# A gather of the expert tables is issued only when the fourth gather ahead of it in the stream has landed

## The chip, the core and the metric

One core of one Trainium2 chip. The metric is the device time of one execution in microseconds. The kernel before took 3083.66 us (median of three runs, 3082.61 to 3083.81).

## What is computed

One layer of a diffusion backbone over 1024 latent tokens of width 1024, with 256 context tokens. A token mixer (attention with 8 heads and a bidirectional recurrent group) is followed by a channel mixer that retrieves single-neuron experts from two tables of 16384 rows of 1024 float32 values, `u` and `v`. Eight heads pick 16 experts each, so 128 rows of each table for every token:

```python
idx = jnp.take_along_axis(cand_i, pos, axis=-1)          # (128 tokens, 8 heads, 16)
g = jax.nn.softmax(top_s, axis=-1)
act = jax.nn.gelu(jnp.einsum('nhkd,nd->nhk', u[idx], xc))
return jnp.einsum('nhk,nhkd->nd', g * act, v[idx])
```

Everything is float32. The layer works on the tokens in 8 chunks of 128.

## The kernel before

The program is written engine by engine, with semaphores set by hand. SP loads and stores plain data. DVE, ACT and PE do the mixer of chunk c + 2 while the experts of chunks c + 1 and c are gathered and used. Once the prelude is over, POOL (GpSimd) does nothing but issue gathers.

A gather (`gather`, L618) is an indirect DMA that takes one row of 4 KB for each of 128 partitions, 524 KB in all, into one place of `ring`, which has `RING` = 11 places. For each chunk there are 128 gathers from `u` and 128 from `v`, 2048 in all, and they form one stream with fixed places:

- a **u gather** j brings the j-th expert of each of the 128 tokens. DVE multiplies it by the tokens and sums along the row (`u_slots`, L1561, one product of 128 x 1024 at L1565);
- a **v gather** j brings the 128 experts of one token, one on each partition. ACT makes a column of weights for it (L960), PE multiplies and adds it into PSUM (`v_slots`, L2092, matmuls at L2100).

The order of the stream is set by `u_place` and `v_place`: for chunk 0 first its 128 u gathers; then for each chunk c 60 v gathers in a row (`lead_gathers`, `LEAD` = 60), then a mixed stretch (`mixed_gathers`) of 16 blocks of twelve, each with 8 u gathers of chunk c + 1 and 4 v gathers of chunk c (`RUN` = 4), then 4 v gathers (`TAIL`). For the last chunk all 128 v gathers stand in a row.

Each ring place r has a semaphore `got[r]`, which a gather raises by 16 when it has landed. DVE and PE wait on it in `landed` (L315). In the other direction DVE raises `u_used` and PE `v_used` for each gather that was used. Ahead of each gather POOL calls `freed` (L638), which waits until the gather 11 places earlier in the stream was used. A gather is issued as soon as that has happened and POOL has finished the one before; how many are in flight at once is limited by the ring alone. Ahead of the first u gather of each half chunk and the first v gather of each chunk POOL also waits for the indices and raises `passed`.

On DVE and PE the uses are woven into the attention work of a later chunk by hand: the mixer code calls `fill(b)` at fixed points, and `fill` runs the uses up to a given place. Both engines work strictly in the written order. So a use that waits for its gather holds up the attention work behind it, and attention work holds up the uses behind it and with them the ring places that these would free.

Of the kernel before, what the change touches and what calls it, by code (L numbers as in the profile page):

```python
# [54 lines left out]
SLOTS = PH * TOPK  # L55
HALF_SLOTS = SLOTS // 2
RING = 11
QUADS, QP = 4, 32
SELS = 8
LABEL = 2 * NK  # L60
# [5 lines left out]
STRIDE = 2 * SLOTS  # L66
# [42 lines left out]
def layer(nc, t):  # L109
    with ExitStack() as ctx:  # L110
# [3 lines left out]
        def sem(name):  # L114
            return ctx.enter_context(nc.semaphore(name))
# [31 lines left out]
        def view(n, *dims):  # L147
            assert at[0] + n <= ARENA, at[0] + n
            a = arena[:, at[0]:at[0] + n]
            at[0] += n  # L150
            if dims:
                names = "abcd"[:len(dims)]
                a = a.rearrange("p (%s) -> p %s" % (" ".join(names), " ".join(names)),
                                **dict(zip(names, dims)))
            return a
# [72 lines left out]
        wo = view(KT * D, KT, D)  # L228
        ring = view(RING * D, RING, D)
        xm_new, xm_next, xm_cur = (view(D) for _ in range(3))  # L230
# [84 lines left out]
        def landed(eng, c, place):  # L315

            r = slot(c, place)
            eng.wait_ge(got[r], 16 * ((c * STRIDE + place) // RING + 1))
            return r

        def slot(c, place):

            return (c * STRIDE + place) % RING

# [28 lines left out]
            "ffn_sd", "ffn_out",  "out_ready", "out_stored")}  # L353
        got = [sem(f"got{r}") for r in range(RING)]

# [210 lines left out]
        def _(pool):  # L566
# [55 lines left out]
            def u_gather(c, j):  # L622

                if j % HALF_SLOTS == 0:
                    pool.wait_ge(S["idx_ready"], 2 * c + j // HALF_SLOTS + 1)
                    pool.sem_inc(S["passed"], 1)
                freed(c, u_place(c, j))
                gather("u", idx_u, j, slot(c, u_place(c, j)))

            def v_gather(c, j):  # L630

                if j == 0:
                    pool.wait_ge(S["idxT_copied"], c + 1)
                    pool.sem_inc(S["passed"], 1)
                freed(c, v_place(c, j))
                gather("v", idx_v[c % 2], token(j), slot(c, v_place(c, j)))

            def freed(c, place):  # L638

                place -= RING  # L640
                first, last = isinstance(c, int) and c == 0, isinstance(c, int) and c == NX - 1
                if first and place < SLOTS:
                    if place >= 0:
                        pool.wait_ge(S["u_used"], place + 1)
                    return
                if place < SLOTS:
                    c, place = c - 1, place + STRIDE
                    last = False
                n = place - SLOTS - LEAD
                if n < 0 or last:  # L650
                    pool.wait_ge(S["v_used"], c * SLOTS + LEAD + n + 1)
                elif n >= MIXED:
                    pool.wait_ge(S["v_used"], c * SLOTS + SLOTS - TAIL + n - MIXED + 1)
                elif n % (3 * RUN) >= 2 * RUN:
                    j = LEAD + RUN * (n // (3 * RUN)) + n % (3 * RUN) - 2 * RUN
                    pool.wait_ge(S["v_used"], c * SLOTS + j + 1)
                else:
                    j = 2 * RUN * (n // (3 * RUN)) + n % (3 * RUN)
                    pool.wait_ge(S["u_used"], c * SLOTS + (SLOTS + j + 1))
# [1033 lines left out]
        def _(pe):  # L1693
# [267 lines left out]
            def spread(b, r, ready):  # L1961

                for i in range(2):
                    ins = M(bank(b + i), lhsT=ident[r:r + 1, r:r + 1].broadcast_to([1, P]),  # L1964
                            rhs=rows[r:r + 1, 512 * i:512 * i + 512], start=True, stop=True)
                ins.then_inc(S[ready], 1)
# [125 lines left out]
            def v_slots(c, lo, hi):  # L2092

                for j in range(lo, hi):
                    q, i = j % QUADS, j // QUADS
                    pe.wait_ge(S["sel_ready"], c * SLOTS + j + 1)
                    r = landed(pe, c, v_place(c, j))
                    for b in range(2):
                        g = (q + 2 * b) % QUADS
                        ins = M(bank(4 + b)[QP * g:QP * g + QP, :], lhsT=sel[:, j % SELS, :],  # L2100
                                rhs=ring[:, r, 512 * b:512 * b + 512], start=(i == 0), stop=(i == QP - 1))
                    ins.then_inc(S["v_used"], 1)
# [85 lines left out]
            spread(0, G2, "g2_ready")  # L2188
            v_slots(NX - 1, G2_AT, SLOTS - RING)
            pe.wait_ge(S["out_ready"], NX - 1)  # L2190
# [55 lines left out]
```

## Time and profile before

| | |
|---|---|
| median of the runs shown | 3083.66 us |
| span of the profiled execution | 3447.3 us |
| POOL busy in the span | 2087.7 us (61%) |
| PE busy | 2466.8 us (72%) |
| DVE busy | 2047.0 us (59%) |
| ACT busy | 785.3 us (23%) |
| read from HBM and written to it | 337 GB/s over the span |

The profiled execution is longer than the unprofiled ones by 363.6 us. All rows of the trace are from that one execution. In a timeline row the first number is the start in us from the span's start, the second the length, and the bracket at the end gives the engine's idle time just before the instruction and what ended it. "remote" there is a release whose sender the trace does not name; "issue" means that no wait shows. DMA landings have no rows of their own, but a DVE or PE row with "<-DMA" started when its gather had landed.

### The profile page before, as it was taken

Reading aid. Unit: us, or ns where it says so; the run is one execution under the profiler, and the core shown is the slowest. Engines: PE = TensorE matmul, PEld = TensorE weight load, DVE = VectorE, ACT = ScalarE, POOL = GpSimd, SP = SyncE. Lnnn points to the kernel's source line nnn. Section 1 sums busy time; section 2 is a strip of 40 time slices with the busy share of each in tenths; the row PEclk is TensorE's granted clock in tenths of the full one; section 3 lists DMA queues with packets and bytes.
Section 4 is the critical chain, followed back from the end, with each engine's and each line's share of the span. In section 5 each row is a group of like instructions: output and inputs, shape, how many; then the busy total and the mean of one; then the engine's idle time right before and its main releaser. Section 6 shows DMA issues by size and latency. Waiting matters only on the chain.

```text
span 3447.3 us, 29321 instructions
## 1 busy us (share of the span) xinstructions
PE 2466.8 (72%) x9222; PEld 1078.6 (31%) x9222; DVE 2047.0 (59%) x4621; ACT 785.3 (23%) x1888; POOL 2087.7 (61%) x2167
## 2 busy tenths in 40 slices
PE   7978977768676776677777867787767766533476
PEld 4844654324221432134222422143213422000011
DVE  4785786666655666656656566665665666565300
ACT  2265111122112221222122221222122212100121
POOL 6910254566666666666666666666666666666665
PEclk8989987886789667865797578956796688855699
DMA  8533499799999999999999999999999999999998
GB/s 319 179 140 113 142 337 358 288 358 362 349 371 367 360 364 367 362 368 358 364 367 375 361 364 372 372 358 366 364 361 370 361 355 359 372 379 368 364 367 323
DMA packets 335937, 1163.76 MB, mean 338 GB/s; under 512 B 40485, under 2 KB 51365, under 8 KB 333608
## 3 DMA queue, kind: packets, MB, share of 16 engines
q0 software_dynamic: 297792, 1084.36, 83.6%
q1 hardware_dynamic: 37994, 77.54, 6.3%
q8 instruction: 76, 1.25, 0.1%
q14 instruction: 75, 0.61, 0.0%
HBM read 1148.13 MB, written 13.63 MB: 337 GB/s over the span
## 4 chain that ended last, share of the span: by engine, by line
PE 29%; POOL 16%; issue 14%; another core or an unknown queue 13%; DMA 12%; DVE 11%; ACT 4%; SPq 1%; DVEq 0%; ACTq 0%; POOLq 0%
POOL arena L619 16%; DMA arena<-in_v,arena 9%; PE psum L2100 9%; DVE arena L1565 6%; PE psum L1931 4%; PE psum L1899 4%; DMA arena<-in_u,idx_u 2%; PE psum L2034 2%; PE psum L1920 2%; PE psum L1946 2%; PE psum L1781 1%; PE psum L1956 1%; PE psum L1980 1%; ACT arena L883 1%
## 5 line engine op out<-in xcount | busy, mean ns | idle before, releaser
L1565 DVE CUSTOM_DVE_ANT_0 arena<-arena,psum 128x1024 f32<-128x1024 f32 x1024 | 1215.6, 1218 | 413.3 <-DMA arena<-in_u,idx_u 379.4
L619 POOL DMA_INDIRECT arena<-in_u,idx_u x1024 | 960.0, 937 | 652.8 <-issue 267.8
L2100 PE MATMUL psum<-arena 128*32 128x512 f32 x4096 | 1013.0, 744 | 445.6 <-DMA arena<-in_v,arena 305.4
L619 POOL DMA_INDIRECT arena<-in_v,arena x1024 | 977.6, 955 | 522.1 <-issue 256.8
L2100 PEld LDWEIGHTS psum<-arena 128*32 128x32 f32 x4096 | 181.8, 124 | 1185.3 <-issue 1036.6
L960 ACT ACTIVATE arena<-arena 128x32 f32<-128x32 f32 x1024 | 277.6, 314 | 1166.4 <-PE psum L2100 580.1
L1899 PE MATMUL psum<-kT,arena 64*128 64x512 f32 (+1 forms) x384 | 252.4, 810 | 56.2 <-issue 26.9
L1920 PE MATMUL psum<-ident,arena 128*128 128x128 f32 x560 | 137.5, 378 | 174.5 <-issue 110.3
L1401 DVE TENSOR_REDUCE small<-psum 128x1 f32<-128x1280 f32 x64 | 95.4, 1491 | 278.4 <-remote 220.8
L1931 PE MATMUL psum<-v,arena 128*128 128x64 f32 x1120 | 230.4, 395 | 27.3 <-ACT arena L883 24.0
L2034 PE MATMUL psum<-wbig,arena 128*128 128x512 f32 x512 | 242.4, 628 | 4.5 <-issue 3.4
L1931 PEld LDWEIGHTS psum<-v,arena 128*128 128x128 f32 x1120 | 221.4, 304 | 45.4 <-ACT arena L883 38.5
L883 ACT ACTIVATE arena<-psum 128x512 f32<-128x512 f32 x168 | 87.9, 523 | 403.6 <-remote 287.1
L1920 PEld LDWEIGHTS psum<-ident,arena 128*128 128x128 f32 x560 | 82.7, 186 | 296.6 <-issue 196.6
L1899 PEld LDWEIGHTS psum<-kT,arena 64*128 64x128 f32 x384 | 100.7, 279 | 185.7 <-issue 147.7
L2034 PEld LDWEIGHTS psum<-wbig,arena 128*128 128x128 f32 x512 | 100.7, 202 | 142.1 <-issue 140.3
L1426 DVE TENSOR_SCALAR small<-small 128x1 f32<-128x1 f32 x24 | 3.6, 152 | 225.8 <-ACT arena L977 164.4
L1964 PE MATMUL psum<-rows,ident 1*128 1x512 f32 x128 | 60.2, 824 | 77.9 <-issue 42.7
L1980 PE MATMUL psum<-arena 128*128 128x512 f32 x224 | 115.0, 668 | 0.0
L826 ACT ACTIVATE arena<-psum,small 128x64 f32<-128x64 f32 x64 | 20.0, 313 | 309.0 <-remote 197.5
L819 ACT ACTIVATE arena<-psum,small 128x1280 f32<-128x1280 f32 x64 | 84.8, 1325 | 23.6 <-issue 13.2
L1565 DVE DVE_READ_ACCUMULATOR2_ANT arena<- 128x1 f32 x1024 | 84.6, 83 | 0.0
(268 smaller groups left out, 2154.9 us busy)
## 6 DMA issues: line engine op xcount, KB each, us to landing
arena<-in_u,idx_u POOLq DMA_INDIRECT x1024
arena<-in_v,arena POOLq DMA_INDIRECT x1024
arena<-in_w_mod POOLq DMA_DIRECT2D x20, 512.0 KB, 4.3
wbig<-in_wq SPq DMA_DIRECT2D x1, 7168.0 KB, 19.7
arena<-in_w_mod SPq DMA_DIRECT2D x12, 512.0 KB, 4.1
arena<-in_xin SPq DMA_DIRECT2D x5, 1024.0 KB, 9.6
arena<-in_w_mod SPq DMA_DIRECT2D x2, 2048.0 KB, 10.7
wbig<-in_w_mod SPq DMA_DIRECT2D x2, 2048.0 KB, 20.5
```

The lines of the kernel that those rows point to most:

```text
L619: pool.indirect_dma_start(ring[:, r, :], None, t[table], bass.IndirectOffsetOnAxis(idx[:, j:j + 1], 0)).then_inc(got[r], 16)
L819: A(pr, psum[:, score_at(n):score_at(n) + KEYS], ACT.Exp, scale=HD ** -0.5, bias=small[:, a:a + 1], accum_out=small[:, b:b + 1]).then_inc( ...
L883: A(pT[:, 4 * g:4 * g + k, :], bank(3)[:, 0:k * P], ACT.Copy).then_inc(S["pt_out"], 1)
L960: A(sel[:, j % SELS, :], hot[:, QP - 1 - i:2 * QP - 1 - i], ACT.Copy, scale=wT[:, n:n + 1])\
L1401: ch.link(V.tensor_reduce(small[:, a:a + 1], psum[:, score_at(n):score_at(n) + KEYS], AX, ALU.max))
L1565: V.tensor_tensor_reduce(ring[:, r, :], ring[:, r, :], hx_cur, 1.0, 0.0, ALU.mult, ALU.add, act_[:, j:j + 1]).then_inc(S["u_used"], 1)
L1899: ins = M(psum[:, at_ + b:at_ + b + w], lhsT=qc[o:o + 64, h // 2, :], rhs=kT[o:o + 64, b:b + w], start=True, stop=True)
L1920: ins = T(bank(3)[:, j * P:(j + 1) * P], pr[:, kt * P:(kt + 1) * P], ident[:, :])
L1931: ins = M(pv, lhsT=pT[:, kt, :], rhs=v[:, kt, 64 * (h % 2):64 * (h % 2) + 64], start=(kt == 0), stop=(kt == NTOK - 1))
L1980: return M(bank(i), lhsT=att[:, kt, :] if kt < 4 else lc[:, kt - 4, :], rhs=wo[:, kt, 512 * i:512 * i + 512], start=(kt == 4), stop=(kt == 3))
L2034: ins = M(bank(i), lhsT=hxT[:, kt, :], rhs=wq[:, kt, 512 * i:512 * i + 512], start=(kt == 0), stop=(kt == KT - 1))
L2100: ins = M(bank(4 + b)[QP * g:QP * g + QP, :], lhsT=sel[:, j % SELS, :], rhs=ring[:, r, 512 * b:512 * b + 512], start=(i == 0), stop=(i == ...
```

## The change

`freed` gets one wait more, at its head. `before` is the place in the stream of the gather four places ahead of the one to be issued, and POOL waits until the semaphore of its ring place says that it has landed. The wait for the ring place 11 earlier stays as it is. Nothing else changes: order, ring size, and all consumers stay.

```diff
 RING = 11
+FLIGHT = 4
 QUADS, QP = 4, 32
@@
             def freed(c, place):
 
+                before = c * STRIDE + place - FLIGHT
+                if before >= 0:
+                    pool.wait_ge(got[before % RING], 16 * (before // RING + 1))
                 place -= RING
```

## Rows read from the trace of the kernel before

**Rows 1.** The page: span, and busy time of each engine with its share.
```profile
span 3447.3 us, 29321 instructions
...
PE 2466.8 (72%) x9222; PEld 1078.6 (31%) x9222; DVE 2047.0 (59%) x4621; ACT 785.3 (23%) x1888; POOL 2087.7 (61%) x2167
```

**Rows 2.** DMA, 374 to 3447 us: gathers' queue, packets, MB, share of 16 engines.
```profile
q0 software_dynamic: 294912, 1073.87, 92.7%
```

**Rows 3.** Groups of instructions: busy us, mean ns of one, idle before, releaser.
```profile
L619 POOL DMA_INDIRECT arena<-in_u,idx_u x1024 | 960.0, 937 | 652.8 <-issue 267.8
...
L619 POOL DMA_INDIRECT arena<-in_v,arena x1024 | 977.6, 955 | 522.1 <-issue 256.8
```

**Rows 4.** Waits: who waited for what, us in total, times, longest us.
```profile
DVE arena L1565 <- DMA arena<-in_u,idx_u: 379.4, 95, 9.6
...
POOL arena L619 <- PE psum L2100: 259.6, 171, 20.1
...
POOL arena L619 <- remote: 187.2, 82, 4.9
...
POOL arena L619 <- DVE arena L1565: 148.5, 116, 23.1
```

**Rows 5.** Timeline of POOL, 1989 to 2008 us, a block of the mixed stretch.
```profile
1989.80 0.93 POOL L619 DMA_INDIRECT arena<-in_u,idx_u  x1 [0.30 <-issue]
...
1997.25 0.94 POOL L619 DMA_INDIRECT arena<-in_u,idx_u  x1 [0.30 <-issue]
2000.94 0.94 POOL L619 DMA_INDIRECT arena<-in_u,idx_u  x1 [2.75 <-remote]
2002.18 0.94 POOL L619 DMA_INDIRECT arena<-in_v,arena  x1 [0.30 <-issue]
...
2007.15 0.94 POOL L619 DMA_INDIRECT arena<-in_u,idx_u  x1 [0.30 <-issue]
```

**Rows 6.** Timeline of DVE, 1996 to 2015 us: uses of the u gathers.
```profile
1996.29 1.22 DVE L1565 CUSTOM_DVE_ANT_0 arena<-arena,psum 128x1024 f32<-128x1024 f32 x1 [3.54 <-issue]
...
2005.38 1.22 DVE L1565 CUSTOM_DVE_ANT_0 arena<-arena,psum 128x1024 f32<-128x1024 f32 x1 [0.42 <-DMA arena<-in_u,idx_u]
...
2013.62 1.22 DVE L1565 CUSTOM_DVE_ANT_0 arena<-arena,psum 128x1024 f32<-128x1024 f32 x1 [7.01 <-DMA arena<-in_u,idx_u]
...
2014.90 1.22 DVE L1565 CUSTOM_DVE_ANT_0 arena<-arena,psum 128x1024 f32<-128x1024 f32 x1
```

**Rows 7.** Timelines of POOL and PE from 3419 us: the last gathers and their uses.
```profile
3419.36 0.94 POOL L619 DMA_INDIRECT arena<-in_v,arena  x1 [1.88 <-PE psum L2100]
3420.60 0.94 POOL L619 DMA_INDIRECT arena<-in_v,arena  x1 [0.30 <-issue]
...
3430.53 0.94 POOL L619 DMA_INDIRECT arena<-in_v,arena  x1 [0.30 <-issue]
...
3426.27 1.05 PE L2100 MATMUL psum<-arena 128*32 128x512 f32 x4 [1.30 <-DMA arena<-in_v,arena]
...
3436.78 1.05 PE L2100 MATMUL psum<-arena 128*32 128x512 f32 x4 [0.18 <-DMA arena<-in_v,arena]
```

**Rows 8.** Timeline of POOL: the second gather, and one behind two waits.
```profile
375.40 0.96 POOL L619 DMA_INDIRECT arena<-in_u,idx_u  x1 [0.30 <-issue]
...
2133.44 0.94 POOL L619 DMA_INDIRECT arena<-in_v,arena  x1 [0.30 <-issue]
```

**Rows 9.** Timelines of POOL and DVE, 962 to 973 us: a lone gather.
```profile
962.02 0.94 POOL L619 DMA_INDIRECT arena<-in_u,idx_u  x1 [0.30 <-issue]
967.80 0.93 POOL L619 DMA_INDIRECT arena<-in_u,idx_u  x1 [4.85 <-PE psum L2100]
...
972.10 1.22 DVE L1565 CUSTOM_DVE_ANT_0 arena<-arena,psum 128x1024 f32<-128x1024 f32 x1 [2.75 <-DMA arena<-in_u,idx_u]
```

**Rows 10.** DMA packets, 1996 to 2001 us, then 2003.5 to 2009 us.
```profile
DMA packets 575, 2.09 MB, mean 419 GB/s; under 512 B 64, under 2 KB 64, under 8 KB 575
...
DMA packets 451, 1.65 MB, mean 300 GB/s; under 512 B 48, under 2 KB 48, under 8 KB 451
```

## The prediction

> **What bounds the kernel now.** Read the totals first. POOL, which only issues gathers from 374 us on, is busy 61% of the span, PE 72%, DVE 59% [rows 1]: none of them is full. The DMA engines are: from 374 us to the end the gathers' queue moves 1073.87 MB and occupies 92.7% of the sixteen engines [rows 2]. That is 2048 gathers of 524 KB. The groups of instructions say that POOL spends 0.94 us on one [rows 3], and the timeline shows 0.30 us between two, so POOL can issue one in 1.243 us (1989.80 to 1997.25 is six of them, 1.242 each [rows 5]). The first issue is at 374.03 (1.37 us before the second [rows 8]), the last at 3430.53 [rows 7], so the mean spacing is 3056.5 / 2047 = 1.493 us. The other 0.25 us each, some 510 us in all, are stalls. The waits name them: POOL waited 259.6 us for PE, 187.2 us for a release without a name and 148.5 us for DVE [rows 4], 595.3 us with the usual 0.30 us before each of those 369 issues in it. They are waits for a free place in the ring of 11.
>
> So two things take turns: the ring that comes free late, and the DMA. What the DMA does between stalls decides this case.
>
> **How many gathers are in flight now.** This is read off by pairing issues with first uses. In the block shown, eight u gathers start at 1989.80 and later, the eighth at 2000.94 after a stall of 2.75 us, then four v gathers from 2002.18, then the next block at 2007.15 [rows 5]. DVE takes the u gathers in order: the first at 1996.29, the eighth at 2005.38, the first of the next block at 2013.62 [rows 6]. From issue to use that is 6.49 us, 4.44 us and 6.47 us. At the end of the stream PE uses every v gather as it lands: the last is issued at 3430.53 and used at 3436.78, 6.25 us [rows 7]. At 1.243 us spacing 6.25 us are 5.0 gathers between issue and use. The change allows four. So it binds wherever POOL runs freely: use of the fourth gather ahead is 6.25 us after its issue, and four spacings are 4.97 us. Only after a stall (4.44 us) is it already fulfilled.
>
> **What the change removes, adds and moves.** It removes nothing. It adds one wait on POOL ahead of 2044 of the 2048 gathers. *The instruction itself:* the second gather, which waits for nothing, starts 0.30 us after the one before it ended; the gather at 2133.44, the first v gather of a chunk, stands behind two waits and a semaphore increment, all fulfilled, and starts 0.30 us after too [rows 8]. A fulfilled wait therefore costs nothing that shows. Bounds 0 and 0.06 us; I take 0: POOL has 0.25 us per gather to spare, which covers it.
>
> *The wait when it is not fulfilled:* the spacing cannot be below a quarter of the time from issue to the moment when POOL sees the landing. I take the time to the consumer's start for that, since POOL wakes on the same semaphore as DVE and PE. From below: a gather with next to nothing ahead of it, issued at 967.80, 5.78 us after the one before it, is used at 972.10, 4.30 us later [rows 9]; 4.30 / 4 = 1.08 us, less than POOL's own 1.243, so the wait would cost nothing. From above: 6.25 / 4 = 1.56 us. In between the queue decides: fewer gathers ahead, less time. The gather issued at 3420.60, second after a stall and so with two to three ahead of it, is used at 3426.27, 5.67 us [rows 7] (nine issues and nine uses from there to the end, one for one). That is the state the cap keeps, three ahead, so I take 5.67 / 4 = **1.42 us**.
>
> Does the DMA lose speed there, or does it merely wait less? In a free run use follows use at 1.28 us (2013.62 to 2014.90), but from the eighth u gather (2005.38) to the ninth (2013.62), five gathers, 8.24 us pass, 1.65 each, though POOL issued these every 1.24 us [rows 5, 6]. The DMA rate says the same: 419 GB/s from 1996 to 2001 us, 300 GB/s from 2003.5 to 2009 [rows 10]. With two gathers ahead of a new one the sixteen engines aren't kept full; with four or five they are. Three is between, and the mean of 1.65 and 1.28, 1.46, is near the 1.42 above.
>
> **Queues behind the wait.** Behind POOL's wait stand only further gathers. DVE's products (u) and PE's sums (v) wait for them, and behind these the attention work of the chunk two ahead. DVE already waited 379.4 us for u gathers [rows 4], so a later u gather delays it directly. A v gather's release of its ring place follows the landing, so POOL's ring waits move too.
>
> **The sum, against the profiled execution.** Span 3447.3 = 374.0 before the stream + 3056.5 + 16.8 after. In the mixed stretches (16 blocks of twelve in each of seven chunks, 112 blocks) a block takes 2007.15 - 1989.80 = 17.35 us now. Capped, twelve spacings of 1.42 are 17.04 us: POOL's stall of 2.45 us at its end would swallow all of it. But the eight u gathers come later one after the other by up to 8 x (1.42 - 1.243) = 1.4 us, and DVE takes them as they land. With half of that passed on, 0.7 us x 112 = **+78 us**; bounds 0 and +157.
>
> The median is 3083.66 us, 363.6 less than the span. Nothing shows where the difference lies; if outside the stream nothing changes, the unprofiled spacing is (3083.66 - 390.8) / 2048 = 1.315 us, and if everything shrinks alike, 1.493 x 0.8945 = 1.336 us. Either is so near the 1.28 of the free run that few stalls can be left to hide the cap. Then the cost is (1.42 - 1.336) x 2048 = **+172 us** to (1.42 - 1.315) x 2048 = **+215 us**, mean 194. I put the forecast midway between 78 and 194, +136 us: **3220 us**, own range 3110 to 3300.
>
> **Rivals.**
> *The DMA stays full (no change).* For it: in the worst trough it is still at 300 GB/s, and a lone gather needs 4.30 us, of which four in flight make 1.08 us. Then 1.243 and not the cap sets the spacing, 3084 us. Against it: 6.25 us is what a gather takes in a free run, and 1.65 spacing after a stall. A variant is that the change does nothing, because four are never exceeded; the 5.0 above speaks against it.
> The Trainium skill, "DMA: Bandwidth & Descriptors", section "Anatomy of one DMA — SWDGE (gpsimd) path", gives 2.0 us + bytes / 436 GB/s for such a transfer. By it a gather would take an estimated 3.2 us and four in flight would allow one in 0.8 us: it would make this rival the forecast. The trace's lone gather, 4.30 us to its use, is longer, and its 6.25 us in a free run is longer still.
>
> *Evenness (faster).* Today a stall drains the queue and the next five gathers take 8.24 us where 5 x 1.28 = 6.4 would do. If POOL, held back evenly, arrives at the release with less run ahead and the trough goes, up to 1.8 us a block come back; 112 x 1.8 = 206 us at most in the profiled execution, of which the unprofiled spacing leaves about a fifth, 40 us: 3044 us. It needs the trough to come from POOL's burst; but the trough follows a release time set by PE, which the cap doesn't move. It decides only if the capped spacing is under 1.31 us.
>
> *Latency doesn't fall with the queue (much slower).* Then 1.56 us: (1.56 - 1.336) x 2048 = +459 us at most, 3543 us; a half-way case at 1.47 gives +274, 3358 us. For it: gathers issued a little after a stall are back at 6.2 us soon (the one at 2007.15). Against it: those had caught up to four ahead again.
>
> **Chances and range.** Forecast 0.63; much slower 0.11; DMA full or no effect 0.15; faster 0.11. A difference of 0.2% (6 us) is about what a measurement of this kernel can tell from none, so faster 0.11, same 0.15, slower 0.74. The range leaves out the faster case below 3080 and the much slower one above 3350.
>
> **What would show it.** After: POOL's idle before L619 put down to the DMA, in hundreds of us; spacing of free runs 1.40 to 1.45 instead of 1.243, issue to use 5.6 to 5.8 instead of 6.25; DVE's wait for u gathers up; the DMA's share and GB/s from 374 us on down by 3 to 6%; ring waits on PE shorter. If instead free runs stay at 1.25 to 1.28 and the last gather is used about 5.2 us after its issue, the DMA stayed full with a shorter queue and the forecast is wrong. It is also wrong if time from issue to use is shorter when nothing is profiled: at 5.3 us the cap gives 1.33, no cost.

## The result

The change made the kernel **18.4% slower**: 3649.32 us (median of four runs, 3647.93 to 3651.09) against 3083.31 us, ratio 1.1835 with a 95% interval of 1.182 to 1.1849. The forecast was 3220 us, with 3080 to 3350 as its range. The direction was right, and the size was wrong by a factor of four: +566 us, not +136.

One thing has to be said before any number is compared. The chips used here fall into two groups. On one kind the kernel before takes 3079 to 3087 us, on the other 3421 to 3452 us. Going by these numbers, the times of before are from the first kind, and the profile shown ahead of the prediction (span 3447.3) is from the second. The experiments e1 and e17 below show that a profiled execution takes what the other executions on its chip take. The trace of the changed kernel, and below a second trace of the kernel before (span 3082.4), are from the first kind. I call them 3082-chips and 3440-chips. The experiments used three of the first (labels e5 to e8, e13 to e16, e17 and e18) and two of the second (e1 to e4, e9 to e12); each was used for one set of runs only, so whether a chip always stays in its group is not known.

The traces of the two kinds differ in one thing more. Those of the 3082-chips record nearly every update that a DMA makes to a semaphore (35225 in e17). Those of the 3440-chips record well under half (12496 in the profile ahead of the prediction, 13249 in e1). So on a 3440-chip a release can lack a name ("remote") because its record is missing, and waits put down to a DMA are counted too low there. The times at which POOL issued are complete in both.

The profile after: gathers (L620 is L619 of before), with POOL's idle time and what ended it.

```profile
L620 POOL DMA_INDIRECT arena<-in_u,idx_u x1024: 932/936/1881, 374.9 to 3419.3; - x171
L620 POOL DMA_INDIRECT arena<-in_v,arena x1024: 932/936/2127, 619.2 to 3632.0; - x171
its engine sat idle before it (us, times) until:
  DMA arena<-in_u,idx_u: 566.7, 826
  DMA arena<-in_v,arena: 555.2, 871
...
DMA to landing us min/median/max: 4.2/6.0/15.4
```

The numbers after x1024 are the shortest, median and longest issue in ns and the first and last start. POOL spent 0.94 us on an issue as before [rows 3], so it isn't slower at its work. But the idle time before 1697 of 2048 issues is put down to a landing, 1121.9 us in all. Each of them contains the usual 0.30 us, 509 us together, so some 610 us are really lost to landings. Before, no issue waited for a landing. The last line gives the time from a gather's issue to its last landing.

The same view of the kernel before on a 3082-chip (label e17):

```profile
L619 POOL DMA_INDIRECT arena<-in_u,idx_u x1024: 935/941/1887, 374.9 to 2890.7; - x171
L619 POOL DMA_INDIRECT arena<-in_v,arena x1024: 935/941/1926, 598.6 to 3062.3; - x171
its engine sat idle before it (us, times) until:
  issue: 461.7, 1515
  DVE arena L1565: 153.7, 267
  PE psum L2100: 129.7, 265
...
DMA to landing us min/median/max: 4.3/9.7/24.7
```

From first to last issue the spacing is (3062.3 - 374.9) / 2047 = 1.313 us before and (3632.0 - 374.9) / 2047 = 1.591 us after. The difference, 0.278 x 2047 = 569 us, is the result. Outside the stream little moved: the first issue is at 374.9 in both, and after the last issue 17.0 us follow instead of 20.1. And the kernel before had 9.7 / 1.313 = 7.4 gathers in flight, not five.

The users waited more, too (the waits of after: DVE and PE for gathers):

```profile
DVE arena L1569 <- DMA arena<-in_u,idx_u: 893.4, 485, 7.6
...
PE psum L2104 <- DMA arena<-in_v,arena: 809.0, 596, 14.0
```

DVE's wait was 379.4 us in the trace ahead of the prediction [rows 4] and is 465.1 us in e17; PE's is 425.7 us in e17. The DMA in both, from 374 us to the end, first e17, then after (packets and rate, and the gathers' queue):

```profile
DMA packets 304901, 1098.44 MB, mean 406 GB/s; under 512 B 33664, under 2 KB 36736, under 8 KB 304768
...
q0 software_dynamic: 294912, 1073.87, 98.0%
```

```profile
DMA packets 304916, 1098.56 MB, mean 335 GB/s; under 512 B 33664, under 2 KB 36736, under 8 KB 304768
...
q0 software_dynamic: 294912, 1073.87, 91.5%
```

The same bytes at 335 instead of 406 GB/s. The share of the engines fell far less than the rate, from 98.0% to 91.5%. The rest is in the packets, which took longer: by these lines 98.0% of 16 engines over 2708 us for 294912 packets make 144 ns each, and 91.5% over 3275 us make 163 ns. So a high busy share of the DMA is no proof that it runs at its full rate.

A free run of POOL in the kernel before (e17) and a stretch of the mixed part of after, as timelines:

```profile
1803.27 0.94 POOL L619 DMA_INDIRECT arena<-in_u,idx_u  x1 [0.30 <-issue]
1804.51 0.94 POOL L619 DMA_INDIRECT arena<-in_u,idx_u  x1 [0.30 <-issue]
1805.76 0.94 POOL L619 DMA_INDIRECT arena<-in_v,arena  x1 [0.30 <-PE psum L2100]
```

```profile
2329.72 0.94 POOL L620 DMA_INDIRECT arena<-in_u,idx_u  x1 [0.30 <-DMA arena<-in_v,arena]
2331.96 0.94 POOL L620 DMA_INDIRECT arena<-in_u,idx_u  x1 [1.30 <-DMA arena<-in_v,arena]
2333.29 0.94 POOL L620 DMA_INDIRECT arena<-in_u,idx_u  x1 [0.40 <-DMA arena<-in_u,idx_u]
2334.80 0.94 POOL L620 DMA_INDIRECT arena<-in_u,idx_u  x1 [0.57 <-DMA arena<-in_u,idx_u]
2336.05 0.94 POOL L620 DMA_INDIRECT arena<-in_u,idx_u  x1 [0.30 <-DMA arena<-in_u,idx_u]
2337.64 0.94 POOL L620 DMA_INDIRECT arena<-in_u,idx_u  x1 [0.66 <-DMA arena<-in_u,idx_u]
```

Before, one issue follows another after 1.24 us. After, the gap of 0.30 us is often 0.4 to 1.3, five issues in 7.92 us, 1.58 each, and each gap ends with a landing.

### The profile page after: what moved, and what is told of

Same layout as the page of the kernel before. It is cut to its first block, busy times and chain, and to the rows that moved or that the text cites. A ratio compares the mean times of both kernels' runs of the same rounds, so it can differ in the third digit from the quotient of the medians.

```text
span 3649.0 us, 31358 instructions
## 1 busy us (share of the span) xinstructions
PE 2485.4 (68%) x9222; PEld 965.9 (26%) x9222; DVE 2069.8 (57%) x4621; ACT 830.0 (23%) x1888; POOL 2091.9 (57%) x2167
## 3 DMA queue, kind: packets, MB, share of 16 engines
q8 instruction: 76, 1.25, 0.1%
## 4 chain that ended last, share of the span: by engine, by line
DMA 28%; POOL 27%; issue 21%; PE 11%; DVE 11%; ACT 2%; SPq 1%; POOLq 1%; DVEq 0%; ACTq 0%
POOL arena L620 27%; DMA arena<-in_u,idx_u 21%; DVE arena L1569 8%; DMA arena<-in_v,arena 6%; PE psum L2104 2%; PE psum L1785 2%; PE psum L2038 2%; PE psum L1950 1%; PE psum L1960 1%; PE psum L1903 0%; SPq L383 0%; PE psum L1722 0%; PE psum L1890 0%; DMA arena<-in_k_norm_g 0%; PE psum L1984 0%
## 5 line engine op out<-in xcount | busy, mean ns | idle before, releaser
L2104 PE MATMUL psum<-arena 128*32 128x512 f32 x4096 | 1211.0, 754 | 839.8 <-DMA arena<-in_v,arena 809.0
L1569 DVE CUSTOM_DVE_ANT_0 arena<-arena,psum 128x1024 f32<-128x1024 f32 x1024 | 1239.6, 1220 | 905.5 <-DMA arena<-in_u,idx_u 893.4
L620 POOL DMA_INDIRECT arena<-in_u,idx_u x1024 | 960.0, 937 | 738.8 <-DMA arena<-in_u,idx_u 337.6
L620 POOL DMA_INDIRECT arena<-in_v,arena x1024 | 982.2, 959 | 633.4 <-DMA arena<-in_v,arena 311.6
L964 ACT ACTIVATE arena<-arena 128x32 f32<-128x32 f32 x1024 | 314.5, 319 | 1635.5 <-PE psum L2104 1635.0
L2104 PEld LDWEIGHTS psum<-arena 128*32 128x32 f32 x4096 | 193.9, 120 | 1785.6 <-issue 1216.5
L1903 PE MATMUL psum<-kT,arena 64*128 64x512 f32 (+1 forms) x384 | 211.0, 698 | 52.6 <-ACT arena L823 51.4
L1935 PE MATMUL psum<-v,arena 128*128 128x64 f32 x1120 | 153.3, 298 | 26.9 <-ACT arena L887 26.9
L1935 PEld LDWEIGHTS psum<-v,arena 128*128 128x128 f32 x1120 | 145.5, 211 | 40.5 <-ACT arena L887 39.1
L1924 PE MATMUL psum<-ident,arena 128*128 128x128 f32 x560 | 112.8, 324 | 54.6 <-ACT arena L887 35.7
L1903 PEld LDWEIGHTS psum<-kT,arena 64*128 64x128 f32 x384 | 86.9, 242 | 160.6 <-issue 100.1
L1924 PEld LDWEIGHTS psum<-ident,arena 128*128 128x128 f32 x560 | 68.2, 159 | 144.9 <-issue 75.9
```

Of the source, the lines that this page charges most:

```text
L620: pool.indirect_dma_start(ring[:, r, :], None, t[table], bass.IndirectOffsetOnAxis(idx[:, j:j + 1], 0)).then_inc(got[r], 16)
L964: A(sel[:, j % SELS, :], hot[:, QP - 1 - i:2 * QP - 1 - i], ACT.Copy, scale=wT[:, n:n + 1])\
L1569: V.tensor_tensor_reduce(ring[:, r, :], ring[:, r, :], hx_cur, 1.0, 0.0, ALU.mult, ALU.add, act_[:, j:j + 1]).then_inc(S["u_used"], 1)
L1903: ins = M(psum[:, at_ + b:at_ + b + w], lhsT=qc[o:o + 64, h // 2, :], rhs=kT[o:o + 64, b:b + w], start=True, stop=True)
L1924: ins = T(bank(3)[:, j * P:(j + 1) * P], pr[:, kt * P:(kt + 1) * P], ident[:, :])
L1935: ins = M(pv, lhsT=pT[:, kt, :], rhs=v[:, kt, 64 * (h % 2):64 * (h % 2) + 64], start=(kt == 0), stop=(kt == NTOK - 1))
```

## The experiments

**Theory A:** the stream is a loop. A gather is issued when the one F ahead has landed, so F x spacing = time from issue to last landing + the time POOL needs to react. **Theory B:** the added wait costs POOL time at each gather. **Theory C:** late gathers delay the attention work on DVE and PE, and that work delays the stream.

### How the two times of before go together: e1 and e17

No edit.

> The kernel before, unchanged. It asks how long a profiled execution of it takes by its own clock, since the profile shown spans 3447 us while its runs take 3083, and the changed kernel's span and runs are both 3649. If the profiler slows a stream with many gathers in flight, this profile again spans over 3400 us and the run takes 3083. If the profile shown was an accident, the span is near 3083.

> The kernel before. Where it takes 3082 us: spacing 1.27 us in the bulk, some 120 intervals over 1.3 us, 6.2 to 6.5 us from issue to landing, POOL's waits for PE released without delay. Where it takes 3440: a third copy of the profile shown.

e1 took 3444.64 us with a span of 3442.8, beside seven runs of the kernel before of 3421 to 3452; e17 took 3084.25 us with a span of 3082.4. So neither of e1's expectations about the profiler held: a profiled execution takes what a run takes, and the chips differ. In e17 the issues came as expected (110 intervals over 1.3 us), but the time from issue to landing, 9.7 us, was far over the 6.2 to 6.5 expected. On the 3440-chip of the first trace the intervals between issues exceed 1.243 us by 515 us in sum, in e17 by 144 us. POOL's named waits for PE, DVE and unnamed senders were 595.3 us there [rows 4] and are 283.4 us in e17 (129.7 for PE and 153.7 for DVE). In the record of semaphore updates of the 3440-chips, PE's releases of several v gathers often come together, 0.06 us apart: four at 2000.68 to 2000.86, of matmuls that began between 1995.73 and 1998.29, and POOL's issue at 2000.94 [rows 5] follows. In that trace 344 of 920 recorded releases by PE come less than 0.15 us after the one before, in e17 58 of 1024. From the start of a gather's last matmul to the next recorded release it is 1.9 us in the median there and 0.61 us in e17. Why PE's releases are late there, no run here shows. That the slow chips are also the ones whose traces lose records leaves open that recording and slowness have one cause; every execution here has its span recorded, so none can tell.

### The limit: e2, e3, e4, e8, e9, e13, e14, e15, e18, e5

```diff
-FLIGHT = 4
+FLIGHT = 3        # and 5, 6, 8, 11
```

> Five instead of four gathers in flight. Theory A (spacing = time from issue to POOL's sight of the landing, divided by the gathers allowed): with four allowed that time is 4 x 1.57 = 6.3 us; with five it is at most 6.3 + 0.6, so 1.26 to 1.38 us of spacing against 1.315 before: 3040 to 3220 us, most likely 3110. Theory B (the added wait costs POOL time at each gather, whatever it waits for): again near 3649 us. Theory C (the cost grows slowly with the limit because engines drift apart): 3300 to 3400 us.

> Eight in flight. Theory A: 6.9 / 8 = 0.9 us, no bound: within 0.3% of 3083 us. Theory B: near 3649 us. A third possibility, that deep queues are needed to fill holes after PE's stalls, gives 3100 to 3150 us.

> Eleven in flight: the wait is for the gather whose ring place is reused, whose use POOL waits for anyway, so it is always fulfilled when its turn to count comes. It prices the instruction alone. Theory A: within 0.2% of 3083 us (0 to 6 us). Theory B: 3649 us. If a fulfilled wait costs POOL 0.06 us and POOL were the bound, 3083 + 0.06 x 2048 = 3206 us.

> The changed kernel (four in flight) again, unchanged. Its own runs were 3649 us beside 3083 us for the kernel before, but on the chip of the second set of experiments the kernel before takes 3446. If the chip slows every gather alike, this takes 3649 x 3446 / 3083 = 4079 us. If only a deep queue is slower on that chip and a stream held to four in flight is bound by time from issue to landing, it takes 3630 to 3670 us on either chip.

> Three in flight. If the spacing is the loop from issue over landing to next issue divided by the number allowed, 6.26 us now with four; with three the queue is shorter by one (0.3 to 0.6 us), so 5.7 to 6.0 us / 3 = 1.9 to 2.0 us: 390 + 2048 x 1.95 = 4380 us (4280 to 4490). If the DMA's speed falls with a shorter queue further than that, over 4490; if the cost is mainly one of the wait, 3700 to 3800.

> Five in flight again, since the first time the kernel before took 3446 us on that chip. Where it takes 3082 us: theory A (spacing = loop from issue over landing to the next issue, over the number allowed; 5.64 us with three, 6.36 with four): about 6.9 / 5 = 1.38 with the same growth, less as the engines fill up; the kernel before has 1.274 in the bulk. 3100 to 3220 us, most likely 3140. If the cost of a separate wait instruction ahead of the ring releases were the main thing, three, four and five would cost alike. If the chip is the slow kind again, 3506.

> The changed kernel. Where the kernel before takes 3082 us: 3645 again. Where it takes 3440: theory A says that the capped stream is bound by its own loop of 6.3 us, which needs neither PE nor DVE, so again 3630 to 3700 us. If everything is slower there, about 4070 us.

> Five in flight. Where the kernel before takes 3082 us: 3100 to 3220 us, most likely 3140 (loop of 6.6 to 6.9 us over five, 1.32 to 1.38 us of spacing). Where it takes 3440: 3507 as twice before.

> Eleven in flight, the ring wait as an instruction of its own. Where the kernel before takes 3082 us there are few stalls on the ring (119 intervals over 1.3 us in the trace of the swapped kernel, against 249 on the other kind), so 0.38 us at each is at most 45 us, and the queue that is full hides most of it: 3083 to 3105 us. Where it takes 3440: 3508 again.

> Six in flight. Where the kernel before takes 3082 us: loop of 7.0 us over six is 1.17 us, under POOL's own 1.243, so within 0.3% of 3083 us. Where it takes 3440: 3507, as five and eight.

On 3082-chips, with spacing from first and last issue and the median from issue to last landing:

| gathers in flight | time us | ratio to before (95%) | spacing us | x limit us | issue to landing us |
|---|---|---|---|---|---|
| 3 (e8) | 4239.03 | 1.375 (1.3722 to 1.3777) | 1.880 | 5.64 | 5.2 |
| 4 (e13) | 3646.58 | 1.1831 (1.1811 to 1.185) | 1.590 | 6.36 | 6.0 |
| 5 (e14) | 3159.89 | 1.0257 (1.024 to 1.0274) | 1.352 | 6.76 | 6.0 |
| 6 (e18) | 3096.64 | 1.0043 (1.0026 to 1.006) | 1.320 | 7.92 | 7.2 |
| 11 (e15) | 3083.78 | 1.0006 (0.9996 to 1.0016) | 1.312 | - | 9.2 |
| no limit (e17) | 3084.25 | the kernel before | 1.313 | - | 9.7 |

e5 gave 3644.67 us with four (1.182, 1.1801 to 1.184), on another chip than e13. Theory B falls: with eleven the same instructions stand in the program and nothing is lost. Theory A holds at three and four: the loop is the landing time (5.25 and 5.97 us) plus 0.39 us. The semaphore record gives the reaction itself: in the changed kernel POOL's issue follows the last landing by 0.259 us, from the fifth percentile to the median; the rest is issues that waited for something else or for POOL's own 1.24 us. At five the loop binds part of the time, at six hardly. I had expected 3140 us for five (3159.89 measured) and 3083 for six (3096.64, outside the 0.3% given), 4280 to 4490 for three (4239.03, below): the direction of the growth is right, but the landing time jumps between three and four and again after five, which a straight line through it doesn't have.

More on it is in the semaphore record. A landed gather has raised its semaphore by sixteen single updates, one for each of the sixteen DMA engines. In medians after the issue, in us (without the first 200 gathers, 1847 in each trace):

| limit | first engine | 15th | last engine |
|---|---|---|---|
| 3 (e8) | 3.84 | 5.06 | 5.25 |
| 4 (after) | 4.19 | 5.71 | 5.97 |
| 6 (e18) | 4.99 | 6.63 | 7.17 |
| none (e17) | 4.83 | 6.87 | 9.73 |

Without a limit the engines drift apart: the first is done with a gather 4.9 us ahead of the last, and the last is 2.9 us behind the fifteenth. The 4.9 us are nearly four gathers at the 1.25 us spacing of the free runs. With four in flight the spread is 1.8 us, and the next issue waits for the last engine. That the lost rate comes from engines that ran out of work while the last one finished is what this suggests. It can't be all of it: by the DMA's lines for the gathers' queue (374 to 3000 us in e8, e14 and e18) the busy share is 83.2% at three, 91.5% at four, 97.4% at five and 98.1% at six, while a packet's mean time is 175, 163, 147 and 144 ns. So part of the loss is idle engines and part is packets that took longer, and what lengthens these no run shows. No run took the drift away without also changing the limit, so its part is argued, not shown. What is shown is the loop: the limit, the time to the last landing that goes with it, and the spacing that follows.

On 3440-chips the row looks different: 3506.21 us with five (e2), 3513.24 with eight (e3), 3508.26 with eleven (e4) and 3508.01 with five again (e9), all 2% above before (1.0206, 1.0221, 1.0195, 1.0213, with 95% intervals from 1.014 to 1.027). The first three had been expected from times of the other kind, at 3110 and 3083 us, and missed. There the limit from five up makes no difference, and something else costs 60 to 75 us. That is the next pair. Whole rows with four in flight were not run on a 3440-chip.

### The wait as an instruction of its own: e6, e7

A gather instruction carries one wait. With two waits ahead of it in the code, the first that stands there goes with the gather, and the other becomes an instruction of its own ahead of it. In the changed kernel that is the ring wait: its trace has a separate instruction for it, and the gather carries the wait for the landing. The edit turns it round.

```diff
             def freed(c, place):
-                before = c * STRIDE + place - FLIGHT
-                if before >= 0:
-                    pool.wait_ge(got[before % RING], 16 * (before // RING + 1))
                 place -= RING
...
                 freed(c, u_place(c, j))
+                landed_ahead(c, u_place(c, j))      # the three lines; v alike
```

> Eleven in flight, with the two waits of a gather the other way round, so that the wait for the ring place is carried by the gather instruction again and the wait for the landing is an instruction of its own. In the kernel with eleven in flight POOL issued 642 ns after a release by PE, before the change 258 ns. If the cost of 62 us is that, paid at each of some 200 stalls (0.38 x 200 = 77 us), it is gone here: within 0.5% of the kernel before. If it is one more instruction per gather (2037 of them), it stays: 1.8 to 2% slower.

> Four in flight, the waits the other way round: now the landing is seen by the separate instruction. If that adds 0.38 us between release and issue, and the landing is what POOL waits for at nearly each gather, the spacing grows by 0.38 / 4 = 0.095 us: 3649 + 195 = 3840 us, less the shorter ring stalls. If the path from release to issue doesn't enter the spacing, no change, 3649.

e7 took 3807.85 us, 4.5% over the unswapped 3644.67 on the same chip (e5), where 3840 was expected. In its semaphore record POOL issues 0.76 us after the last landing instead of 0.26: **0.50 us more**, where 0.38 was expected. The wait instruction for the landing stands between the two. The loop grows by 4 x (1.669 - 1.591) = 0.31 us only, since the landing time falls to 5.7 us. So the path from release to issue is part of the loop, as theory A says. e6 took 3082.3 us (0.9998, 0.9988 to 1.0007). It ran on a 3082-chip, though, where the unswapped order costs nothing either (e15), so e6 doesn't show what e4 lost. The traces of e1 and e4 say what it may have been. At a stall that PE ends, ACT (L960, L964) is released by the same updates as POOL. First e1, then e4, timelines of POOL and ACT:

```profile
997.98 0.94 POOL L619 DMA_INDIRECT arena<-in_v,arena  x1 [2.51 <-remote]
...
997.75 0.53 ACT L960 ACTIVATE arena<-arena 128x32 f32<-128x32 f32 x2 [4.62 <-remote]
```

```profile
1016.49 0.93 POOL L620 DMA_INDIRECT arena<-in_u,idx_u  x1 [10.53 <-PE psum L2104]
...
1015.75 0.53 ACT L964 ACTIVATE arena<-arena 128x32 f32<-128x32 f32 x2 [4.53 <-PE psum L2104]
```

POOL comes 0.23 us after ACT in e1 and 0.74 us after it in e4, medians 0.24 and 0.74 over 48 and 87 stalls. Some 240 intervals between issues are over 1.3 us in either trace; 240 x 0.5 = 120 us is a bound, and the 62 us lost lie within it. That is an argument from size: no run on a 3440-chip had the waits the other way round. On the 3082-chips there are half as many such intervals (110 in e17), and e15 lost nothing to them.

### The cap where there is no attention work: e10, e16

```diff
-                if before >= 0:
+                if before >= (NX - 1) * STRIDE + SLOTS:
```

> The cap of four only where the gather ahead lies in the last chunk's v gathers (124 gathers, no attention work and no u gathers beside them). Theory A: 124 x (1.59 - 1.31) = 35 us, 3117 us (3105 to 3130). If the cost came by way of DVE's and PE's attention work, which is delayed by late gathers, there is none left here: under 3090.

> The cap of four on the last 124 gathers only. Where the kernel before takes 3082 us: 124 x (1.59 - 1.25) = 35 to 42 us, 3117 to 3125 us. Where it takes 3440: 14 us, as before.

e16: 3118.18 us against 3082.6, +35.6 us, ratio 1.0122 (1.0105 to 1.0138), for 124 capped gathers: 0.287 us each, where the whole change costs 566 / 2044 = 0.277. POOL waited 77.0 us for landings, 116 times; without the usual 0.30 us in each that is 42 us:

```profile
  DMA arena<-in_v,arena: 77.0, 116
```

In these 124 gathers neither u gathers nor attention work stand beside the stream, so theory C isn't needed for the cost. On the 3440-chip (e10) it was +17 us (1.0042, 1.0018 to 1.0065), where I had expected 35 from the spacings of the other kind.

### Half the bytes: e11, e12

```diff
+            ch.link(nc.gpsimd.memset(ring[:, :, 512:D], 0.0))
...
-                pool.indirect_dma_start(ring[:, r, :], None, t[table],
+                pool.indirect_dma_start(ring[:, r, 0:512], None, t[table].rearrange("n (h d) -> (n h) d", h=2),
```

These kernels leave out half of the gathered data. An index now picks one of 32768 half rows; it isn't always the first half of the row that it named, but the number of bytes is what counts here. e12 has the cap of four besides.

> The kernel before with gathers of half the size: each row's first 2 KB only, from a table seen as 32768 half rows, so that half the gathered data is left out; DVE and PE work on whole ring places as before, and POOL clears the other halves once. No cap. If POOL's 1.243 us per gather and the engines' uses bound it then: 2930 to 3000 us. It is the partner of the next run.

> The same half rows with the cap of four. It asks what the 5.5 us from issue to landing are made of. If they are mainly other gathers' transfer ahead of one's own (three of about 1.25 us, and its own), half the bytes shorten the loop of 6.3 us to below 5 us, and the spacing is POOL's 1.243 us with or without the cap: within 2% of the run without it. If they are mainly fixed latency, the loop stays over 5.6 us, the spacing over 1.4: over 3250 us, 8% slower than without the cap.

Both ran on a 3440-chip: 3449.64 us without the cap and 3497.92 with it, 1.4% more, beside 3434.55 for the kernel before. I had expected 2930 to 3000 us for e11. Half the bytes gained nothing there, so on these chips the DMA's transfer doesn't bound the kernel. That PE's late releases do instead fits POOL's waits there, but no run took them away. With the cap 22.5 us before 19 issues are put down to landings:

```profile
  DMA arena<-in_u,idx_u: 15.6, 10
  DMA arena<-in_v,arena: 6.9, 9
```

This count is too low, since most landings are missing from the record. The issues are complete, and they say the same: the median interval between two is 1.25 us with the cap and without it. In the semaphore record the time from issue to the last recorded update is 3.4 us in e11, against 6.0 in e1; of the few gathers with at least 14 updates recorded (113 and 149) it is 3.5 and 6.3 us. So over 2.5 of some 6 us go away with half the bytes, and the loop of four, 3.5 + 0.3 = 3.8 us, no longer binds at 0.95 us per gather. The difference of 48 us between the two is of the size of e4's.

## Why the prediction was wrong, point by point

- **What bounds the kernel.** POOL's 1.243 us per gather and 0.94 us of work are confirmed. "Some 510 us of stalls" was right for the trace, but it was a trace of a 3440-chip. On a 3082-chip only 144 us are over 1.243 per gather (e17).
- **Profile against median.** I took the 363.6 us for something the profiler adds. The estimate made from it, 1.315 us "if outside the stream nothing changes", was nevertheless exact (1.313). A step that failed is the one after: I averaged the +194 us that follow from it with +78 us worked out for blocks with stalls that the timed chips hardly have. It took 58 us off the forecast.
- **In flight now.** Five was what the uses in the trace shown gave (6.25 us) and wrong for the timed chips: 9.7 us, 7.4 gathers. Hence the reading that four is nearly enough.
- **The spacing under the cap, the largest error.** I took 5.67 / 4 = 1.42 us from a single gather in the first steps after a stall, and called that state the one that the cap keeps. It is 1.59: 6.0 us to the landing and 0.26 us to the issue, with the rest from issues that wait longer. Even the upper bound of my own pair, 6.25 / 4 = 1.56, was exceeded. That gather had, by my own words, two to three ahead of it. In the changed kernel 1812 of 1848 gathers (without the first 200) were issued with three still in flight, and they took 5.97 us in the median; the 36 with two took 5.47 us, and 5.67 lies between. At 1.59 the same sum gives (1.590 - 1.313) x 2047 = +567 us. Of the 430 us that the forecast lacks, some 350 are this step: (1.59 - 1.42) x 2047.
- **The rivals.** "Latency doesn't fall with the queue", at 0.11, came nearest in its number: 1.56 us against 1.59, and 3543 us "at most" because its spacing before was 1.336. Its mechanism is not what came. On the timed chips the latency did fall with the queue, from 9.7 us without a limit to 6.0 with four and 5.2 with three, only not far enough for four; that 6.25 us from the other kind of chip lies so near the 6.23 us of landing and reaction at four is luck. Its argument had also a reading wrong: the gather issued at 2007.15 was used 6.47 us later, not 6.2. "The DMA stays full" was wrong: the rate fell from 406 to 335 GB/s. The page's figure of the Trainium skill ("DMA: Bandwidth & Descriptors", "Anatomy of one DMA — SWDGE (gpsimd) path"), an estimated 3.2 us for a gather, is again not what the trace has: the shortest from issue to landing is 4.2 us in after and the median 6.0. "Evenness" had nothing to it in the free runs of the timed chips, where there is no trough to fill.
- **The fulfilled wait.** 0 is confirmed on 3082-chips (e15). Left out was the unfulfilled one behind a separate wait instruction, +0.5 us at a stall (e7), which may be the 2% on 3440-chips.
- **Queues behind the wait.** DVE's and PE's waits rose as said, to 893.4 and 809.0 us. But they follow the stream; e16 has the same cost per gather without them.

## What to carry to other kernels

A limit of F transfers in flight costs nothing only if F x the wanted spacing exceeds the time from issue to the *last* engine's landing, plus the issuing engine's reaction. That time is the one that holds at this limit, and it can't be read from the stream without one: here it was 5.2, 6.0, 6.0, 7.2 and 9.7 us with three, four, five, six and no limit. The 9.7 us would have given 2.4 us of spacing at four, and the gather behind a stall gave 1.42; 1.59 was measured. So run one value of the limit before forecasting others. Leave a margin too: with five the medians satisfy the rule (5 x 1.313 = 6.57 us against 6.0 + 0.26), and it still cost 2.6%. Four cost 18% and six 0.4%. Compare the span of a profile with the runs first: where they differ by more than the runs among themselves, the trace may be from another chip, and its stalls are not those of the runs.

## What the runs showed of the hardware

- Two kinds of chips: the same kernel took 3082 us on some and 3421 to 3452 us on others, and on the latter PE's releases come late and bunched and much of the semaphore record is missing; the kernel capped at four was timed on 3082-chips only.
- The sixteen DMA engines finish one 524 KB gather over 1.8 us (four in flight) to 4.9 us (no limit) from first to last, and without a limit the last was 2.9 us behind the fifteenth.
- POOL issues a gather 0.26 us after a release that the gather itself waits for, and 0.76 us after one that a separate wait instruction ahead of it waits for.
- At 91.5% busy share the DMA moved 335 GB/s, at 98.0% 406 GB/s; a gather packet took 163 ns in the mean in the one and 144 ns in the other.
